# A two-block hybrid layer on one Trainium2 core: level exponents of the recurrent mixer by TensorE in place of GpSimd

## The chip, the cores and the metric

One core of a Trainium2 chip runs the whole program. The time is that of the device for one execution, in microseconds (us); the numbers below are medians of several executions. The engines of a core each run their own queue in order and meet at semaphores: TensorE (PE in the profile, with its weight loads as PEld), VectorE (DVE), ScalarE (ACT), GpSimd (POOL) and SyncE (SP), which here issues the transfers.

## The reference

Two layers follow one another on 2048 tokens of width 1024. Only the second one's mixers matter here. It projects x to 3784 columns, then two mixers run: an attention over 256 selected keys per query (4 heads, an index score of 8 heads, a top-k by threshold), and a gated linear recurrence with 4 heads of 128 key and 128 value channels. Of the recurrence:

```python
f = lbh + (1.0 - lbh) * jax.nn.sigmoid(f_raw)      # decay per token, head and key channel
k = 1.0 - f
log_f = jnp.log(f)
bc = jnp.cumsum(log_f, over the tokens of a chunk)
diff = bn[:, :, :, None, :] - bn[:, :, None, :, :]
decay = jnp.exp(jnp.where(causal, diff, -jnp.inf))
scores = einsum('bhtk,bhsk,bhtsk->bhts', qn, kn, decay)
o = scores @ vn + (qn * exp(bn)) @ state
state = exp(b_last) * state + (kn * exp(b_last - bn)).T @ vn
```

The decay between two tokens s < t is different for each key channel, so the scores are no plain matrix product of q and k. Then come an RMS norm, a gate, the output projection and a layer norm.

## The kernel before

The second layer's mixers run in eighteen steps (`second_mixers`, L3456), each closed by a barrier of all engines (`step`, L145). Step k has up to five branches that share no data within the step: index scores of one tile of 128 queries (`index_scores`), the upper half of the search for the threshold (`upper_half`, 16 rounds on VectorE), the lower half (`lower_half`, 16 rounds on ScalarE), the attention of a tile (`attend`) and one chunk of 128 tokens of the recurrence (`hgrn_chunk`, in steps 0 to 15). Tiles are taken from the widest to the narrowest: the last query tile sees 2048 keys, each later step 128 fewer, while a chunk of the recurrence is always the same work. So steps shorten from 123 to 50 us.

Within a step the order on each engine is settled when the program is built. Each branch is written as a generator per engine that yields a place between 0 and 1 before each piece of work (`yield 8.4 / N`), and `together` (L162) puts the pieces of all branches on the engine's queue in order of their places. The recurrence counts its places in 29ths of a step (`N = 29.0`). The queues are in order, so a piece that waits holds up whatever stands behind it.

The recurrence of a chunk divides the pairs s < t into seven levels. At level l blocks of 2 * 2^l tokens are halved; a pair is of that level when s lies in the first half and t in the second. With b the running sum of log f and j the last token of the first half, the decay is exp(b_j - b_s) * exp(b_t - b_j), and both factors are at most 1. So for each level the kernel needs an exponent E for every token and channel: b_j - b_s in first halves, b_t - b_j in second ones. Then:

- TensorE makes b as a product of log f with a matrix of ones (`c.upto`, L3275) in accumulator bank 6, and ScalarE copies it to SBUF (`bT`, L3154).
- GpSimd makes the exponents of a level with two subtractions of 256 columns, `diffs` (L3185, L3186), and b_last - b for the state with one of 512 columns (L3198).
- ScalarE takes the exponential of a level in place (L3158), and those of b_last - b and b (L3162 to L3165).
- GpSimd multiplies first halves with k and second halves with q, `tilde` (L3191, L3192).
- TensorE multiplies the result with itself, per head (L3293), into bank 6 or 7 by turns; that holds the level's scores at the pairs of the level.
- VectorE picks these into A with a mask, `pick` (L3241).

E has two buffers and the banks 6 and 7 serve two levels by turns. In GpSimd's queue the subtractions of level l+1 stand ahead of the products of level l. TensorE writes a bank again when VectorE has picked the level two before.

After the levels the state is read and updated (L3300 to L3312, L3257) and the output is normed. The other branches' work on the same queues: TensorE has index dots (L2718), logits (L3053), turns (L3059) and weighing (L3066); ScalarE has rectifying (L2702), signs (L2814), exponentials (L2961) and copies (L2976); VectorE has the weighted sum of index scores (L2681), counting (L2774 to L2778), and adding the mask and taking the maximum (L2991); GpSimd has the bias (L2942).

A setup (`last_mixers_setup`, L3322) ahead of the eighteen steps loads constants and turns keys.

Of the kernel before, what the change touches and what calls it, by code (L numbers as in the profile page):

```python
# [17 lines left out]
ALU = mybir.AluOpType  # L18
# [3 lines left out]
P = 128  # L22
# [31 lines left out]
BD = 128  # L54
PAD = 4
GROUP = 512
LEVELS = 7
# [39 lines left out]
CONST_COLS = CAUSAL0 + GROUP + 2 * P  # L97

# [2493 lines left out]
HGRN_SIGNALS = ("hx_in hf_ahead sigs h_tanhs h_silus f_done logf turned_hq hq_kept turned_hk hk_kept sums b_kept pairs own_set "  # L2592
# [480 lines left out]
def hgrn_buffers(B, big, y):  # L3073
# [11 lines left out]
    b.bT = B.sb("bT", [P, H, P])  # L3085
# [17 lines left out]
def hgrn_chunk(c, b, s, proj, i):  # L3103
# [5 lines left out]
    lb, g, state, x, k, qT, kT, bT, E, A = b.lb, b.g, b.state, b.x, b.k, b.hqT, b.kT, b.bT, b.E, b.A  # L3109
# [12 lines left out]

    def joint(l):
        half = 1 << l
        v = bT[:].rearrange("p h (n a b) -> p h n a b", a=2, b=half)[:, :, :, 0, half - 1]
        return spread(v, 3, half)
# [10 lines left out]
    def scalar(act):  # L3137
# [16 lines left out]
        act.activation(bT[:], four(6), ACT.Copy).then_inc(s.b_kept, 1)  # L3154
        for l in range(LEVELS):
            yield (6.5 + 2 * l) / N
            act.wait_ge(s.diffs, 2 * (l + 1))
            act.activation(E[:, l % 2], E[:, l % 2], ACT.Exp).then_inc(s.h_exps, 1)  # L3158
            if l == 0:
                yield 7.2 / N  # L3160
                act.wait_ge(s.e_in, 1)
                act.activation(ke[:], ke[:], ACT.Exp)  # L3162
                act.drain()
                act.activation(qe[:], bT[:], ACT.Exp)
                act.activation(dec[:], bT[:, :, P - 1], ACT.Exp).then_inc(s.e_out, 1)  # L3165
# [12 lines left out]
    def gpsimd(pool):  # L3178

        def diffs(l):  # L3180
            if l >= 2:

                pool.wait_ge(s.pairs, l)
            (e0, e1), (b0, b1) = halves(E[:, l % 2], l), halves(bT[:], l)
            pool.tensor_tensor(e0, joint(l), b0, ALU.subtract).then_inc(s.diffs, 1)  # L3185
            pool.tensor_tensor(e1, b1, joint(l), ALU.subtract).then_inc(s.diffs, 1)  # L3186

# [6 lines left out]
        yield 6 / N  # L3194
        pool.wait_ge(s.b_kept, 1)
        diffs(0)

        pool.tensor_tensor(ke[:], spread(bT[:, :, P - 1], 2, P), bT[:], ALU.subtract).then_inc(s.e_in, 1)  # L3198
        for l in range(LEVELS):
            if l + 1 < LEVELS:  # L3200
                yield (7 + 2 * l) / N
                diffs(l + 1)
            yield (7.5 + 2 * l) / N
            tilde(l)
# [409 lines left out]
```

## Time and profile before

| | us |
|---|---|
| median of 3 runs | 5201.58 |
| lowest and highest | 5184.79, 5215.15 |
| span of the profiled execution (first to last instruction) | 5189.6 |
| PE busy | 4361.9 (84%) |
| DVE busy | 2639.9 (51%) |
| ACT busy | 1922.0 (37%) |
| POOL busy | 711.8 (14%) |

The profile gives the profiled execution as its span; what the timed runs have beyond a span (start and end of the execution) is not split off. The shares are means over stages that differ much: the first layer and the two projections are TensorE's, while in the stage that the change touches (3469 to 4932 us of the span) VectorE and ScalarE are busy as well. The mean granted TensorE clock was 0.829 of full speed over the span.

### The profile page before, as it was taken

How to read it: one execution, taken by the hardware profiler on the slowest of the kernel's cores; microseconds unless marked ns; L12 is line 12 of the kernel's file. 1: busy time of each engine (PE TensorE's matmuls, PEld its weight loads, DVE VectorE, ACT ScalarE, POOL GpSimd, SP SyncE). 2: the span in 40 equal slices, each digit the busy share in tenths (PEclk: the TensorE clock that was granted, in tenths of full speed). 3: DMA queues.
4: the chain of work that ended last, by engine and by line, in shares of the span. 5: the costliest groups of instructions: out<-in, count | busy, mean ns of one | idle time of the engine just before them, and what ended most of it. 6: DMA issues, size and time to landing. Idle time of an engine off the chain costs nothing. (4 is left out here: it accounts for less than half of the span.)

```text
span 5189.6 us, 65192 instructions
## 1 busy us (share of the span) xinstructions
PE 4361.9 (84%) x23554; PEld 3247.0 (63%) x23554; DVE 2639.9 (51%) x5371; ACT 1922.0 (37%) x3900; POOL 711.8 (14%) x745
## 2 busy tenths in 40 slices
PE   7997999984688888888898999977787878787679
PEld 6885777774566555656787888853344444454467
DVE  3113444445555544444212111138889888888545
ACT  3112323324323333333101101023667776777621
POOL 3102111100000000000000000003222333344400
PEclk9998999985567777778899999976677788778789
DMA  5327666664000000000423212120000000101033
GB/s 184 119 106 239 210 221 204 215 206 139 28 24 24 24 24 24 13 24 3 154 109 115 82 65 81 55 73 17 19 28 29 19 19 19 37 19 35 31 126 118
DMA packets 203393, 425.84 MB, mean 82 GB/s; under 512 B 37224, under 2 KB 67596, under 8 KB 202908
## 3 DMA queue, kind: packets, MB, share of 16 engines
q1 hardware_dynamic: 203072, 421.67, 23.7%
q8 instruction: 188, 3.08, 0.2%
q14 instruction: 133, 1.09, 0.1%
HBM read 299.93 MB, written 121.65 MB: 81 GB/s over the span
## 5 line engine op out<-in xcount | busy, mean ns | idle before, releaser
L3185 POOL TENSOR_TENSOR ds_E<-ds_bT 128x256 f32<-128x256 f32 x112 | 72.8, 650 | 2797.5 <-ACT ds_bT L3154 2620.6
L2718 PE MATMUL ds_big<-ds_ikT,ds_iqT 64*128 64x512 f32 (+3 forms) x608 | 382.0, 759 | 75.4 <-ACT ds_iqT L2695 54.6
L301 PE MATMUL g_acc<-g_ws_hi,g_hT_hi 128*128 128x512 f32 (+1 forms) x1024 | 386.5, 377 | 0.0
L303 PE MATMUL g_acc<-g_ws_hi,g_hT_lo 128*128 128x512 f32 (+1 forms) x1024 | 384.9, 376 | 0.0
L302 PE MATMUL g_acc<-g_ws_lo,g_hT_hi 128*128 128x512 f32 (+1 forms) x1024 | 384.9, 376 | 0.0
L529 PE MATMUL mm_big<-mm_gw_hi,mm_ghT_hi 128*128 128x512 f32 (+1 forms) x768 | 321.4, 418 | 31.0 <-PEq L134 31.0
L2774 DVE TENSOR_SCALAR_CACHE_REDUCE ds_seen<-ds_eq,ds_num 128x2048 uint16<-128x2048 uint16 (+13 forms) x224 | 331.3, 1479 | 26.4 <-issue 4.4
L531 PE MATMUL mm_big<-mm_gw_hi,mm_ghT_lo 128*128 128x512 f32 (+1 forms) x768 | 302.7, 394 | 0.0
L530 PE MATMUL mm_big<-mm_gw_lo,mm_ghT_hi 128*128 128x512 f32 (+1 forms) x768 | 302.0, 393 | 0.0
L2814 ACT ACTIVATE ds_signs<-ds_lo,ds_at 128x2048 bf16<-128x2048 uint16 (+13 forms) x224 | 291.3, 1301 | 1.5
L328 DVE COPY g_stage<-g_acc 128x512 f32<-128x512 f32 (+1 forms) x64 | 41.5, 649 | 459.2 <-PE g_acc L303 459.2
L2681 DVE SCALAR_TENSOR_TENSOR ds_score<-ds_rel,ds_iw,ds_score 128x512 f32<-128x512 f32 (+3 forms) x266 | 221.3, 836 | 56.5 <-ACT ds_rel L2702 39.8
L1332 PE MATMUL fox_big<-fox_kT,fox_qT 65*128 65x512 f32 (+3 forms) x320 | 223.7, 793 | 29.9 <-PEq L134 29.9
L2718 PEld LDWEIGHTS ds_big<-ds_ikT,ds_iqT 64*128 64x128 f32 x608 | 107.6, 233 | 208.7 <-issue 76.0
L2702 ACT ACTIVATE ds_rel<-ds_big 128x512 f32<-128x512 f32 (+3 forms) x304 | 162.6, 538 | 168.1 <-PE ds_big L2718 89.0
L3293 PEld LDWEIGHTS ds_big<-ds_E 128*128 128x128 f32 x896 | 137.4, 234 | 138.0 <-POOL ds_E L3192 71.5
L347 ACT ACTIVATE g_stage<-g_acc 128x512 f32<-128x512 f32 (+1 forms) x64 | 36.2, 566 | 502.5 <-PE g_acc L303 502.5
L303 PEld LDWEIGHTS g_acc<-g_ws_hi,g_hT_lo 128*128 128x128 f32 x1024 | 193.5, 189 | 35.4
L302 PEld LDWEIGHTS g_acc<-g_ws_lo,g_hT_hi 128*128 128x128 f32 x1024 | 193.7, 189 | 34.9
L301 PEld LDWEIGHTS g_acc<-g_ws_hi,g_hT_hi 128*128 128x128 f32 x1024 | 193.8, 189 | 34.7
L1288 ACT ACTIVATE fox_pT<-fox_big 128x512 f32<-128x512 f32 (+3 forms) x160 | 85.2, 533 | 347.8 <-PE fox_big L1356 347.7
L3066 PE MATMUL ds_big<-ds_pT,ds_ct 128*128 128x128 f32 x1088 | 171.6, 303 | 49.6 <-ACT ds_pT L2976 49.4
(519 smaller groups left out, 10155.1 us busy)
## 6 DMA issues: line engine op xcount, KB each, us to landing
mm_ghT_hi<-turned SPq DMA_DIRECT2D x96, 512.0 KB, 3.8
mm_ghT_lo<-turned SPq DMA_DIRECT2D x96, 512.0 KB, 5.5
proj<-g_stage SPq DMA_DIRECT2D x112, 256.0 KB, 2.0
proj<-mm_gstage SPq DMA_DIRECT2D x80, 256.0 KB, 5.0
mm_x<-proj SPq DMA_DIRECT2D x64, 256.0 KB, 3.8
second_raw<-in_w_in SPq DMA_DIRECT2D x56, 256.0 KB, 4.2
proj<-fp_stage SPq DMA_DIRECT2D x48, 256.0 KB, 2.0
mm_graw<-in_w_in SPq DMA_DIRECT2D x40, 256.0 KB, 6.4
```

What stands on the lines that cost most here:

```text
L301: pe.matmul(sums, hT.hi[:, k, tile], wt.hi[:, k, 0:width], start=(k == 0), stop=False)
L302: pe.matmul(sums, hT.hi[:, k, tile], wt.lo[:, k, 0:width], start=False, stop=False)
L303: mm = pe.matmul(sums, hT.lo[:, k, tile], wt.hi[:, k, 0:width], start=False, stop=(k == KD - 1))
L529: pe.matmul(sums, b.hT.hi[:, u % 3, k], wt.hi[:, k, 0:width], start=(k == 0), stop=False)
L530: pe.matmul(sums, b.hT.hi[:, u % 3, k], wt.lo[:, k, 0:width], start=False, stop=False)
L531: m = pe.matmul(sums, b.hT.lo[:, u % 3, k], wt.hi[:, k, 0:width], start=False, stop=(k == KD - 1))
L1332: pe.matmul(big[:, n, 0:wd], b.qT[:, h, k * P:(k + 1) * P], b.kT[:, h, x:x + wd], start=True, stop=True).then_inc(s.logits, 1)
L2681: d = dve.scalar_tensor_tensor(out=score[:, x:x + wd], in0=rel[:, n % 2, 0:wd], scalar=sg, in1=score[:, x:x + wd], op0=ALU.mult, op1=ALU.add)
L2718: pe.matmul(big[:, n % 2, 0:wd], iqT[o, h // 2], b.ikT[o, x:x + wd], start=True, stop=True)\
L2774: dve.tensor_scalar(seen, hi, cand, 0.0, ALU.is_ge, ALU.add, accum_out=count)
L2814: act.activation(signs, lo, ACT.Sign, bias=now, accum_out=sums[:, bit:bit + 1])
L3066: m = pe.matmul(big[:, 5, h * P:(h + 1) * P], b.ct[:, x // P + t], pT[:, (h * NP + p) % 2, t], start=(p == 0 and t == 0), stop=(x + (t + 1 ...
```

## The change

The exponents of a level no longer come from differences of b. Each is a sum of log f over some tokens: over s+1 to j for a token s of a first half, over j+1 to t for a token t of a second half. So for each level TensorE multiplies log f (as it lies, tokens on the partitions) with a 128 x 128 matrix of zeros and ones. The seven matrices are made on the host, come in as an input `sums` and stay in SBUF. b_last - b is made likewise, with the constant matrix `c.after`. The product goes to bank 6 or 7, the same bank that the level's scores use later; ScalarE reads the exponents there and writes E to SBUF. `bT` and its copy go. In TensorE's queue the exponents of level l+1 stand ahead of the scores of level l, and wait for VectorE's pick of level l-1; that pick moves from place 9.3 + 2l to 7.9 + 2l. ScalarE's exponentials of b and b_last - b come ahead of all levels.

```diff
+def level_sums():
+    s, t = np.arange(P)[:, None], np.arange(P)[None, :]
+    out = []
+    for l in range(LEVELS):
+        half = 1 << l
+        joint = t // (2 * half) * (2 * half) + half - 1
+        out.append(((t < s) & (s <= joint)) | ((joint < s) & (s <= t)))
+    return np.concatenate(out, axis=1).astype(np.float32)
...
     def scalar(act):
         act.wait_ge(s.sums, 1)
-        act.activation(bT[:], four(6), ACT.Copy).then_inc(s.b_kept, 1)
+        act.activation(qe[:], four(6), ACT.Exp)
+        act.activation(dec[:], four(6)[:, :, P - 1], ACT.Exp).then_inc(s.e_out, 1)
+        yield 4.6 / N
+        act.wait_ge(s.e_in, 1)
+        act.activation(ke[:], four(7), ACT.Exp).then_inc(s.ke_kept, 1)
         for l in range(LEVELS):
-            yield (6.5 + 2 * l) / N
-            act.wait_ge(s.diffs, 2 * (l + 1))
-            act.activation(E[:, l % 2], E[:, l % 2], ACT.Exp).then_inc(s.h_exps, 1)
-            if l == 0:
-                yield 7.2 / N
-                act.wait_ge(s.e_in, 1)
-                act.activation(ke[:], ke[:], ACT.Exp)
-                act.drain()
-                act.activation(qe[:], bT[:], ACT.Exp)
-                act.activation(dec[:], bT[:, :, P - 1], ACT.Exp).then_inc(s.e_out, 1)
+            yield (6.6 + 2 * l) / N
+            act.wait_ge(s.diffs, l + 1)
+            act.activation(E[:, l % 2], four(6 + l % 2), ACT.Exp).then_inc(s.h_exps, 1)
...
     def gpsimd(pool):
-        def diffs(l):
-            if l >= 2:
-                pool.wait_ge(s.pairs, l)
-            (e0, e1), (b0, b1) = halves(E[:, l % 2], l), halves(bT[:], l)
-            pool.tensor_tensor(e0, joint(l), b0, ALU.subtract).then_inc(s.diffs, 1)
-            pool.tensor_tensor(e1, b1, joint(l), ALU.subtract).then_inc(s.diffs, 1)
-        yield 6 / N
-        pool.wait_ge(s.b_kept, 1)
-        diffs(0)
-        pool.tensor_tensor(ke[:], spread(bT[:, :, P - 1], 2, P), bT[:], ALU.subtract).then_inc(s.e_in, 1)
         for l in range(LEVELS):
-            if l + 1 < LEVELS:
-                yield (7 + 2 * l) / N
-                diffs(l + 1)
             yield (7.5 + 2 * l) / N
             tilde(l)
         yield 20 / N
-        pool.wait_ge(s.e_out, 1)
+        pool.wait_ge(s.ke_kept, 1)
...
     def vector(dve):
             if l:
-                yield (9.3 + 2 * l) / N
+                yield (7.9 + 2 * l) / N
                 pick(l - 1)
...
+    def diffs(pe, l):
+        if l == 0:
+            pe.wait_ge(s.e_out, 1)
+        elif l == 1:
+            pe.wait_ge(s.own_set, 1)
+        else:
+            pe.wait_ge(s.picked, l - 1)
+        for h in range(H):
+            m = pe.matmul(big[:, 6 + l % 2, h * P:(h + 1) * P], f[:, h * BD:(h + 1) * BD], b.sums[:, l],
+                          start=True, stop=True)
+        m.then_inc(s.diffs, 1)
     def tensor(pe):
         m.then_inc(s.sums, 1)
+        yield 4.2 / N
+        pe.wait_ge(s.hk_kept, 1)
+        for h in range(H):
+            m = pe.matmul(big[:, 7, h * P:(h + 1) * P], f[:, h * BD:(h + 1) * BD], c.after, start=True, stop=True)
+        m.then_inc(s.e_in, 1)
         yield 5 / N
-        pe.wait_ge(s.hk_kept, 1)
+        diffs(pe, 0)
+        pe.wait_ge(s.ke_kept, 1)
         for h in range(H):
             m = pe.matmul(big[:, 7, h * P:(h + 1) * P], kT[:, h], qT[:, h], start=True, stop=True)
         m.then_inc(s.pairs, 1)
         for l in range(LEVELS):
+            if l + 1 < LEVELS:
+                yield (8.2 + 2 * l) / N
+                diffs(pe, l + 1)
             yield (8.4 + 2 * l) / N
             pe.wait_ge(s.tilde, 2 * (l + 1))
-            if l == 0:
-                pe.wait_ge(s.b_kept, 1)
-            elif l == 1:
-                pe.wait_ge(s.own_set, 1)
-            else:
-                pe.wait_ge(s.picked, l - 1)
...
 def last_mixers_setup(nc, c, w, proj, table, onehot, sums, ib, tb, ab, hb):
             sp.dma_start(hg[:], row(w['hgrn_norm_g_2'])).then_inc(s.lb_in, 16)
+            sp.dma_start(hb.sums[:].rearrange("p l t -> p (l t)"), sums).then_inc(s.rest_in, 16)
```

## Rows read from the trace of the kernel before

**Rows 1.** Windows by step: stretch, length, busy PE, PEld, DVE, ACT, POOL, clock, DMA.
```profile
3763.00:3886.00 123.00, 104.04 (x420) 59.53 (x420) 108.80 (x188) 88.18 (x156) 35.52 (x38) 0.79 0.06 20
...
4000.00:4116.00 116.00, 97.33 (x385) 55.73 (x385) 100.94 (x182) 81.40 (x149) 34.66 (x40) 0.77 0.07 24
...
4746.50:4817.00 70.50, 48.85 (x236) 34.54 (x236) 56.11 (x147) 51.19 (x124) 31.73 (x38) 0.81 0.09 31
4817.00:4882.00 65.00, 39.44 (x208) 31.89 (x208) 44.41 (x133) 45.02 (x115) 31.41 (x39) 0.74 0.09 33
4882.00:4932.00 50.00, 28.30 (x135) 21.69 (x133) 16.73 (x41) 38.16 (x97) 27.29 (x35) 0.66 0.11 38
...
sum 1511.00, PE 1158.77 PEld 702.42 DVE 1232.47 ACT 1016.99 POOL 531.46; mean PE 68.16 PEld 41.32 DVE 72.50 ACT 59.82 POOL 31.26
```

**Rows 2.** Waits, 3540 to 4595 us: waiter, releaser, total us, times, longest.
```profile
DVE ds_score L2681 <- ACT ds_rel L2702: 18.9, 16, 3.8
...
PE ds_big L2718 <- ACT ds_iqT L2695: 43.9, 10, 5.2
PE ds_big L3019 <- PEq L134: 34.1, 11, 5.3
```

**Rows 3.** Groups by form, GpSimd: shapes xcount, busy us, mean ns, idle before.
```profile
L3186 POOL TENSOR_TENSOR ds_E<-ds_bT 128x256 f32<-128x256 f32 x112 | 76.4, 682 | 0.0
L3185 POOL TENSOR_TENSOR ds_E<-ds_bT 128x256 f32<-128x256 f32 x112 | 72.8, 650 | 2797.5 <-ACT ds_bT L3154 2620.6 <-PE ds_big L3293 176.8
...
L3198 POOL TENSOR_TENSOR ds_ke<-ds_bT 128x512 f32<-128x512 f32 x16 | 18.6, 1162 | 0.0
```

**Rows 4.** VectorE: groups by form, then timeline (start us, us, engine, line).
```profile
L2681 DVE SCALAR_TENSOR_TENSOR ds_score<-ds_rel,ds_iw,ds_score 128x512 f32<-128x512 f32 x196 | 180.4, 923 | 49.0 <-ACT ds_rel L2702 37.8 <-issue 0.6
L2778 DVE SCALAR_TENSOR_TENSOR ds_num<-ds_num 128x1 f32<-128x1 f32 x224 | 54.4, 243 | 19.4 <-issue 3.0
...
3950.99 0.16 DVE L2778 SCALAR_TENSOR_TENSOR ds_num<-ds_num 128x1 f32<-128x1 f32 x1
...
3951.61 0.61 POOL L3185 TENSOR_TENSOR ds_E<-ds_bT 128x256 f32<-128x256 f32 x1 [3.53 <-PE ds_big L3293]
...
3951.80 0.97 DVE L2681 SCALAR_TENSOR_TENSOR ds_score<-ds_rel,ds_iw,ds_score 128x512 f32<-128x512 f32 x1
...
3956.60 0.73 DVE L2681 SCALAR_TENSOR_TENSOR ds_score<-ds_rel,ds_iw,ds_score 128x512 f32<-128x512 f32 x1
```

**Rows 5.** Groups by form, ScalarE: a level's exponential and the copy.
```profile
L3158 ACT ACTIVATE ds_E<-ds_E 128x512 f32<-128x512 f32 x112 | 69.9, 624 | 4.7 <-POOL ds_E L3186 2.9
...
L3154 ACT ACTIVATE ds_bT<-ds_big 128x512 f32<-128x512 f32 x16 | 9.5, 596 | 4.1 <-PE ds_big L3275 3.4
```

**Rows 6.** TensorE's level scores: group by form, and two of them in the timeline.
```profile
L3293 PE MATMUL ds_big<-ds_E 128*128 128x128 f32 x896 | 158.5, 332 | 60.7 <-POOL ds_E L3192 40.1 <-DVE ds_A L3241 20.3
...
3950.37 1.16 PE L3293 MATMUL ds_big<-ds_E 128*128 128x128 f32 x8
...
4777.33 2.08 PE L3293 MATMUL ds_big<-ds_E 128*128 128x128 f32 x8 [1.79 <-POOL ds_E L3192]
```

**Rows 7.** Timeline, step from 3886: scores of level 4, pick of level 3.
```profile
3960.27 1.16 PE L3293 MATMUL ds_big<-ds_E 128*128 128x128 f32 x8
...
3963.13 0.74 DVE L3241 COPY_PREDICATED ds_A<-consts_sb,ds_big 128x512 f32<-128x512 uint32 x1
```

**Rows 8.** Timeline, last recurrent step, around the exponential of the last level.
```profile
4925.53 1.02 PE L3053 MATMUL ds_big<-ds_cT,ds_ql 128*128 128x512 f32 x2
...
4926.11 0.63 ACT L3158 ACTIVATE ds_E<-ds_E 128x512 f32<-128x512 f32 x1 [1.40 <-POOL ds_E L3186]
...
4927.53 0.72 POOL L3191 TENSOR_TENSOR ds_E<-ds_E,ds_kT 128x256 f32<-128x256 f32 x1
```

**Rows 9.** Timeline, setup: SyncE's last load and VectorE's last arithmetic.
```profile
3443.21 0.56 SPq L3349 DMA_DIRECT2D ds_uv<-in_w_uv  x1
...
3471.16 0.42 DVE L3390 TENSOR_SCALAR ds_hg<-ds_hg 128x512 f32<-128x512 f32 x1
```

More of the change, by code:

```diff
@@ L2591 @@
                   "o_kept o_ps y_done ")
-HGRN_SIGNALS = ("hx_in hf_ahead sigs h_tanhs h_silus f_done logf turned_hq hq_kept turned_hk hk_kept sums b_kept pairs own_set "
+HGRN_SIGNALS = ("hx_in hf_ahead sigs h_tanhs h_silus f_done logf turned_hq hq_kept turned_hk hk_kept sums ke_kept pairs own_set "
                 "diffs h_exps tilde picked e_in e_out ee_done ke_t ktok_done ho_ps up_ps sqd rs hy_done ")
@@ L3084, in hgrn_buffers @@
     b.hqT = B.sb("hqT", [P, H, P])
-    b.bT = B.sb("bT", [P, H, P])
+    b.sums = B.sb("hsums", [P, LEVELS, P])
     b.E = B.sb("E", [P, 2, H, P])
@@ L3108, in hgrn_chunk @@
     H = BH
-    lb, g, state, x, k, qT, kT, bT, E, A = b.lb, b.g, b.state, b.x, b.k, b.hqT, b.kT, b.bT, b.E, b.A
+    lb, g, state, x, k, qT, kT, E, A = b.lb, b.g, b.state, b.x, b.k, b.hqT, b.kT, b.E, b.A
     qe, ke, ktok, dec, ss, big = b.qe, b.ke, b.ktok, b.dec, b.ss, b.big
@@ L3121, in halves @@
         return v[:, :, :, 0], v[:, :, :, 1]
[L3123 to L3126, printed above, removed]
     def sync(sp):
@@ L3316, in hgrn_chunk, with last_mixers_setup @@
     return {"sync": sync, "gpsimd": gpsimd, "vector": vector, "scalar": scalar, "tensor": tensor}
-def last_mixers_setup(nc, c, w, proj, table, onehot, ib, tb, ab, hb):
+def last_mixers_setup(nc, c, w, proj, table, onehot, sums, ib, tb, ab, hb):
     R, big = P, hb.big
@@ L3351, in _ @@
             sp.dma_start(table, ot).then_inc(s.table_out, 16)
-            sp.wait_ge(s.rest_in, n + 32)
+            sp.wait_ge(s.rest_in, n + 48)
             sp.wait_ge(s.table_out, 16)
@@ L3453, with second_mixers @@
 LAST_SIGNALS = "pw_in0 pw_in1 pw_in2 pw_hi pw_lo "
-def second_mixers(nc, c, w, proj, mix, table, onehot, x_old, out):
+def second_mixers(nc, c, w, proj, mix, table, onehot, sums, x_old, out):
     H, R, KEEP = 4, 128, float(TOPK)
@@ L3482, in second_mixers @@
         hb = hgrn_buffers(E, big, y)
-        last_mixers_setup(nc, c, w, proj, table, onehot, ib, tb, ab, hb)
+        last_mixers_setup(nc, c, w, proj, table, onehot, sums, ib, tb, ab, hb)
         last = Named()
@@ L3555, in second_mixers, with program @@
         project_out(nc, c, mix, w['w_o_2'], x_old, out, "pf", ln=(w['ln_g_2'], w['ln_b_2']), held=last)
-def program(nc, t, consts, onehot, out):
+def program(nc, t, consts, onehot, sums, out):
     w = {n: (v[0] if v.shape[0] == 1 else v) for n, v in t.items()}
@@ L3583, in program @@
             second_projection(nc, c, x2, w['w_in_2'], proj2, spans((0, COLS2)), raw)
-        second_mixers(nc, c, w, proj2, mixed2, table, onehot, x2, out)
+        second_mixers(nc, c, w, proj2, mixed2, table, onehot, sums, x2, out)
     nc.sync.sem_clear(nc.turns.ranges[1 - nc.turns.now])
@@ L3603 @@
         views[n] = nc.dram_tensor(f"in_{n}", a.shape, F32, kind="ExternalInput").ap()
-    made = {"consts": shape_constants(), "onehot": bucket_table()}
+    made = {"consts": shape_constants(), "onehot": bucket_table(), "sums": level_sums()}
     for n, a in made.items():
@@ L3608 @@
     out = nc.dram_tensor("out", [1, SEQ, D_MODEL], F32, kind="ExternalOutput").ap()
-    program(nc, {n: views[n] for n in INPUTS}, views["consts"], views["onehot"], out)
+    program(nc, {n: views[n] for n in INPUTS}, views["consts"], views["onehot"], views["sums"], out)
     r = run_bass_kernel_spmd(nc, [arrays], core_ids=[0])
```

## The prediction

> **What bounds the kernel now.** The touched code runs only in the last-but-one stage, so I read that first: the busy times of its sixteen recurrent steps [rows 1]. The reader is to see three kinds of step. From 3540 to about 4675 us VectorE is busy for 85 to 91% of each step (100.94 of 116.00 us in one) and TensorE for 75 to 85%; GpSimd, whose work the change removes, has 34.66 us in that step. In the last two, VectorE falls to 44.41 and 16.73 us, and no engine is full: these are bound by latency, by chains that go from engine to engine. Next, who waits: over ten long steps the longest entry of VectorE's waits is 18.9 us in 1055 us [rows 2]. VectorE is the limit there; what shortens VectorE shortens the step, and what shortens GpSimd alone doesn't. Third, TensorE at the start of a step: 43.9 us for ten waits on the turned index queries and 34.1 us for eleven step barriers, so 4.4 + 3.1 = 7.5 us of each step that it can't use [rows 2].
>
> About 0.5%, 26 us, is what a measurement of this kernel tells from no change. The stage is 1463 us long (the 1511 us of the windows less the 48 after the last recurrent step), so it would have to move by 1.8%.
>
> **GpSimd's part that goes.** Per chunk, seven times two subtractions and one wide one: 72.8 + 76.4 + 18.6 = 167.8 us over sixteen chunks [rows 3], 10.5 us a chunk, of GpSimd's 531.46 us in the stage [rows 1]. It is worth something through two doors.
>
> First, VectorE is slower beside GpSimd. VectorE's weighted sum of 512 columns takes 0.73 us with GpSimd quiet and 0.97 us when issued 0.19 us behind a GpSimd subtraction [rows 4]; its mean over 196 is 923 ns, so 196 x 0.193 = 37.8 us are lost to company. A one-column operation takes 0.16 us alone and 243 ns in the mean of 224: 18.6 us more. Together 56 us. The removed instructions are 167.8/531.46 = 32% of GpSimd's time, so 18 us of it, if the loss is spread by time. The other short VectorE operations that are delayed stand at the beginning and end of a step, beside GpSimd work that stays, so I add nothing for them. The lower bound is 0 (the remaining GpSimd work slides into the freed places and hurts as before), the upper one twice, 36 us. Of the 18 us, thirteen of sixteen steps can turn it into time: **-15 us**.
>
> The Trainium skill (SBUF — State Buffer, section Who interferes with whom) has the reason: a VectorE operation with two inputs in SBUF and a GpSimd operation that reads SBUF take a common port pair as an exclusive lock, and the second waits for the first. The 0.97 against 0.73 us agrees. By that rule alone a collision would cost up to a whole GpSimd instruction (0.61 us), where the mean loss here is 0.19 us, as most do not collide. If each removed instruction blocked VectorE for half its length, 84 us would go (an estimate by the page's rule and the lengths in the trace); the 56 us that the rows show for all of GpSimd forbid that.
>
> Second, latency. GpSimd's queue has the subtractions of level l+1 before the products of level l. In the long steps nobody on the path waits for it: 0. In the short ones it shortens a chain, but the exponents then come from another queue (below), so I count 0, bound -1.3 us a step (two subtractions, 0.65 + 0.68) in five steps.
>
> **ScalarE.** One copy of 596 ns goes [rows 5] and one drain; the three exponentials remain, read from the accumulators in place of SBUF. The nearest rows: a copy out of the accumulators takes 596 ns and an exponential in SBUF 624 ns, so I count the new form as the old; bound 28 ns each either way, 0.3 us a chunk. 16 x 0.6 = 9.5 us of an engine that is 70% busy (81.40 of 116.00): 0 on the path, bound -9.5.
>
> **TensorE's part that comes.** Eight groups a chunk (seven levels and the one for the keys' decay), each four products of 128x128x128 in f32, which the trace shows as eight matmuls. The same shape is there: the level scores take 1.16 us a group at the upper clock level (2.4 GHz) and 2.08 us at the lower (1.2 GHz), and 158.5/112 = 1.42 us in the mean [rows 6]. So 8 x 1.42 = 11.3 us a chunk (9.3 at the upper, 16.6 at the lower level), 181 us over the stage. Room: in the step of 116 us TensorE has 97.33 busy and 7.5 shut off, 11.2 us left; in the first with attention at full width 104.04 of 123.00, 11.5 left [rows 1, 2]. It just fits. TensorE isn't at its peak, though: the granted clock is 0.77 to 0.79 in these two, so over 40% of the time it runs at half speed, and work done at that speed would shrink. I take 0.5 us for each of ten long steps for VectorE instructions that are now late behind a full TensorE: **+5 us**; bounds 0 and the rival below.
>
> **The waits that are added.** The products of level l+1 stand at place 8.2+2l of 29 in TensorE's order and wait until VectorE has picked level l-1; VectorE's pick moves from 9.3+2l to 7.9+2l for this. While TensorE waits, index scores, logits and turns queue behind it, and VectorE in the end waits for those. In the step from 3886 (the 114 us up to the one of row 4000): the pick of level 3 started at 3963.13 [rows 7] at place 17.3. A unit is 114/29 = 3.9 us, so 1.4 units earlier is 3957.6, done by 3958.4. TensorE reaches the point just before the scores of level 4, which started at 3960.27; less a group of 1.16 us the new one must begin at 3959.1. The pick comes 0.7 us before that. So the wait is nearly always over, but with little to spare: 0 in the long steps. VectorE's own earlier place is safe: the scores of level 3 started at 3950.37 [rows 6], some 7 us before.
>
> **The short steps.** ScalarE's exponential of a level (place 6.6+2l) is now 0.4 units behind TensorE's products (6.2+2l): 0.7 us in a step of 50 us, less than a group takes. In the last recurrent step: TensorE finished logits at 4925.53 + 1.02 = 4926.55 and would make the last level's exponents then, until 4927.71, while the exponential started at 4926.11 [rows 8]. It would start at 4927.8, GpSimd's products of the level at 4928.5 in place of 4927.53: 1.0 us late, and the level scores after them too. I take +1.0 us for each of the last five steps: **+5 us**; bounds -1.3 (GpSimd's relief counts in full) and +3 (the group at the lower clock level on two levels).
>
> **Beginning.** The matrices come in with one more transfer of 128 x 3584 B = 459 KB in the setup; the queue issued its last load at 3443.21 and VectorE ends the setup 28 us later, at 3471.16 + 0.42 [rows 9]: hidden, 0. It moves six other loads by about the 0.56 us that one issue takes; what ends the setup, VectorE's arithmetic on the bounds, waits for none of them. Bound +0.6.
>
> **Sum.** -15 + 5 + 5 = -5 us. The page gives the span of the profiled execution, 5189.6 us, which would become 5184.6; the median of the timed runs is 12 us above the span, and the difference is what I carry over: 5201.58 - 5 = **5197 us**. No measurable change is likeliest.
>
> **Rival A, slower: TensorE becomes the limit.** If the new groups run at the lower clock level, they add 16.6 us a step. Then TensorE's busy time, the addition and the 7.5 us shut off exceed the step: by 97.33 + 16.6 + 7.5 - 116 = 5.4 us, by 2.5 us in the one of 70.5 us; over the eleven steps from 3763 to 4817 (the first and the last of which stand in [rows 1]) it is 51 us in all. With the +5 of the short steps and no relief, as VectorE isn't the limit then: 5201.6 + 56 = 5258 us. It decides once a group costs more than 1.4 us in these steps (8 x 1.4 = 11.2, the room above). For it: the room is that small. Against it: the scores of levels 3 and 4 in a long step ran at 1.16 us [rows 6, 7]. Halfway, a third of the steps, gives 5225.
> The Trainium skill (TensorE: Matmul & The Clock Gate, What's actually happening) says that the half clock is the default and activity releases it. The clock of 0.77 to 0.79 beside 84% busy doesn't bear that out cleanly; if it holds, 64 more matmuls a step raise the clock and this rival dies.
>
> **Rival B, faster.** The removed subtractions sit between VectorE's densest work, and all of the upper bound counts: -36 us x 13/16 = -29, nothing late on TensorE as more work keeps its clock up, and the short steps gain GpSimd's 1.3 us each: -6.5. Together 5166 us. For it: the 0.97 us stood beside a subtraction that goes [rows 4]. Against it: 531.46 - 167.8 = 364 us of GpSimd's work stay and can collide [rows 1, 3].
>
> **Rival C: it is only moved.** GpSimd's remaining work collides as often as before, TensorE hides everything: 5202 +- 5. It can't be told from my forecast by time.
>
> **Chances.** Forecast with C 0.56, A in whole or part 0.25, B 0.19. These are the chances of same, slower and faster. The range takes in B to 5163 and half of A to 5230.
>
> **What would show it.** VectorE's weighted sum falls from 923 ns towards 850 (right) or stays (C). GpSimd's busy time falls by 168 us. TensorE's rises by 150 to 260 us; the mean of a new group at 1.2 us speaks for B, at 2 us for A, and so does a VectorE that waits over 5 us a step on ScalarE's rectified scores. The last two steps grow by 1 us. I am wrong if TensorE's waits for the pick total over 30 us, or if a long step changes by more than 3 us.

## The result and the profile after

The changed kernel takes 5211.37 us (median of 20 runs, 5197.08 to 5222.88) against 5194.70 us for the kernel before in the same comparison. The ratio is 1.0029 with a 95% interval of 1.0018 to 1.0039: 15 us slower, 9 to 20. The forecast was 5 us faster, no measurable change; the size is below the 26 us that the prediction took for measurable, the sign is wrong, and twenty runs tell it.

First the whole stage, in one window each, from the barrier ahead of the first recurrent step to the one behind the last (length, busy of PE, PEld, DVE, ACT, POOL, clock). In the kernel before that last barrier stands at 4942.6 us. The windows read ahead of the prediction closed the step at 4932, when its state was still being read: it is 61 us long and not 50, and the stage 1470.7 us and not 1463. The kernel before:

```profile
3471.90:4942.60 1470.70, 1139.43 (x4608) 689.20 (x4608) 1215.19 (x2392) 1000.44 (x2046) 525.51 (x604) 0.76 0.07 26
```

The changed kernel:

```profile
3474.90:4966.00 1491.10, 1197.47 (x5632) 793.31 (x5632) 1177.34 (x2392) 991.98 (x2030) 364.20 (x364) 0.81 0.07 25
```

The stage holds the loss: it is 20.4 us longer, of the 24.0 us between the two profiled executions. VectorE, the limit of the long steps, is busy for 37.9 us less, twice what was forecast, and GpSimd for 161 us less. VectorE's idle time rises by 58 us, from 255.5 to 313.8, and eats that and more. TensorE is busy for only 58.0 us more. The new work is far larger than this; the changed kernel's groups by form, TensorE:

```profile
L2730 PE MATMUL ds_big<-ds_ikT,ds_iqT 64*128 64x512 f32 x448 | 298.6, 782 | 70.7 <-ACT ds_iqT L2707 52.6 <-ACT ds_rel L2714 18.0
L3257 PE MATMUL ds_big<-ds_hsums,ds_f 128*128 128x128 f32 x896 | 149.0, 317 | 46.6 <-DVE ds_A L3229 45.7 <-DVE ds_A L3235 0.8
L3296 PE MATMUL ds_big<-ds_E 128*128 128x128 f32 x896 | 139.1, 305 | 8.4 <-POOL ds_E L3188 8.1
L3281 PE MATMUL ds_big<-consts_sb,ds_f 128*128 128x128 f32 x128 | 31.7, 429 | 0.0
```

149.0 + 31.7 = 180.7 us are new, as forecast (181). But the old work shrank, the level scores from 158.5 to 139.1 us [rows 6] and, of others, the index dots from 315.7 us in the kernel before:

```profile
L2718 PE MATMUL ds_big<-ds_ikT,ds_iqT 64*128 64x512 f32 x448 | 315.7, 836 | 70.7 <-ACT ds_iqT L2695 51.5 <-ACT ds_rel L2702 19.1
```

The reader is to see two thirds of the added busy time given back, at a granted clock of 0.81 in place of 0.76. Cut at each change of the granted clock, TensorE's busy time before is 538 us at the lower level and 601 at the upper; after, it is 412 and 785, with 80 and 101 us of the new groups among them. So 206 us of old work left the lower level; taken at half the time on the upper one [rows 6 have 2.08 and 1.16 us], that is some 103 of the 123 us that are missing. The rest is overlap: group by group, busy times add up to 107 us more than the total before, and to 129 us more after. The relief of VectorE, changed kernel, groups by form, against [rows 4]:

```profile
L2693 DVE SCALAR_TENSOR_TENSOR ds_score<-ds_rel,ds_iw,ds_score 128x512 f32<-128x512 f32 x196 | 158.5, 811 | 55.3 <-ACT ds_rel L2714 44.5 <-issue 0.6
L2790 DVE SCALAR_TENSOR_TENSOR ds_num<-ds_num 128x1 f32<-128x1 f32 x224 | 43.6, 194 | 19.1 <-issue 2.6
```

923 ns became 811, 243 became 194. The 923 of this one profile is high, though: five kernels below that keep all of GpSimd's work (twice, twicemid and the three with earlier picks in the kernel before) have 881 to 895. Then who waits for whom (total us, times, longest), first VectorE in the kernel before:

```profile
DVE ds_score L2681 <- ACT ds_rel L2702: 39.8, 31, 3.8
DVE ds_L L2991 <- PE ds_big L3053: 20.8, 24, 2.8
DVE ds_A L3247 <- PE ds_big L3280: 17.4, 8, 8.8
...
DVE ds_A L3241 <- PE ds_big L3293: 11.3, 4, 4.2
```

In the changed kernel VectorE waits for the same four, and others for each other in two new ways:

```profile
DVE ds_score L2693 <- ACT ds_rel L2714: 51.1, 36, 5.3
DVE ds_A L3235 <- PE ds_big L3287: 41.9, 15, 10.5
DVE ds_A L3229 <- PE ds_big L3296: 23.7, 16, 4.2
DVE ds_L L3003 <- PE ds_big L3065: 22.9, 24, 3.3
...
ACT ds_E L3169 <- PE ds_big L3257: 67.1, 35, 4.6
...
PE ds_big L3257 <- DVE ds_A L3229: 45.7, 41, 5.2
```

Own scores (k with q of the same token; L3235 is the line L3247 of before) cost 24.5 us more, picks 12.4, rectified scores 11.3. TensorE's matmuls sit idle 45.7 us in front of the level exponents until a pick, and ScalarE waits 67.1 us for these exponents. Of the wait for picks, most is in the long steps (3540 to 4600 us):

```profile
PE ds_big L3257 <- DVE ds_A L3229: 35.5, 28, 5.2
```

By chunk, the largest change of a single one stands at the beginning. The first chunk, which has index scores beside it and no attention, from barrier to barrier, before and after:

```profile
3471.90:3541.20 69.30, 57.71 (x184) 26.97 (x184) 42.00 (x61) 32.78 (x64) 30.62 (x34) 0.80 0.10 35
```

```profile
3474.90:3550.80 75.90, 66.53 (x248) 36.30 (x248) 40.17 (x61) 32.85 (x63) 19.01 (x19) 0.79 0.09 32
```

6.6 us of the 20 are here, 4.4 in chunks 1 and 2, 7.8 in chunks 11 to 15. Chunks 3 to 10, the long steps from 3763 to 4593, sum up to within 2 us of what they were. Single ones moved by up to 6 us; but chunk 4, which did, is 5 us longer in bpick79 and bpick86 too, so no cause is read from them one by one.

### The profile page after: what moved, and what is told of

It reads as the page before. It is cut to its first block and busy times, and to the rows that moved or that the text cites. A ratio compares the mean times of both kernels' runs of the same rounds, so it can differ in the third digit from the quotient of the medians.

```text
span 5213.6 us, 66857 instructions
## 1 busy us (share of the span) xinstructions
PE 4416.9 (85%) x24578; PEld 3349.1 (64%) x24578; DVE 2604.5 (50%) x5371; ACT 1912.6 (37%) x3884; POOL 551.0 (11%) x505
## 5 line engine op out<-in xcount | busy, mean ns | idle before, releaser
L2730 PE MATMUL ds_big<-ds_ikT,ds_iqT 64*128 64x512 f32 (+3 forms) x608 | 355.6, 697 | 76.0 <-ACT ds_iqT L2707 56.6
L3187 POOL TENSOR_TENSOR ds_E<-ds_E,ds_kT 128x256 f32<-128x256 f32 x112 | 90.6, 809 | 3107.7 <-ACT ds_E L3169 3107.6
L2693 DVE SCALAR_TENSOR_TENSOR ds_score<-ds_rel,ds_iw,ds_score 128x512 f32<-128x512 f32 (+3 forms) x266 | 204.0, 768 | 67.4 <-ACT ds_rel L2714 51.1
L3257 PEld LDWEIGHTS ds_big<-ds_hsums,ds_f 128*128 128x128 f32 x896 | 128.4, 219 | 122.9 <-DVE ds_A L3229 80.4
L1057 PE MATMUL fp_acc<-fp_ws_hi,fp_hT_hi 128*128 128x512 f32 (+1 forms) x528 | 199.0, 377 | 9.0 <-issue 3.9
```

The costliest lines, as they stand in the source:

```text
L1057: pe.matmul(sums, hT.hi[:, j % 3, n], ws.hi[:, n, at], start=(n == 0), stop=False)
L2693: d = dve.scalar_tensor_tensor(out=score[:, x:x + wd], in0=rel[:, n % 2, 0:wd], scalar=sg, in1=score[:, x:x + wd], op0=ALU.mult, op1=ALU.add)
L2730: pe.matmul(big[:, n % 2, 0:wd], iqT[o, h // 2], b.ikT[o, x:x + wd], start=True, stop=True)\
```

## The experiments

All ratios are against the kernel before, run in turns on the same chip; 0.001 is 5.2 us. The medians of the kernel before differ by up to 7 us between comparisons, so only ratios are compared. Two questions came first: is it the load on TensorE, or the waits that come with it?

| kernel | ratio | 95% interval | us against before |
|---|---|---|---|
| the change | 1.0029 | 1.0018 to 1.0039 | +15 |
| twice: load only | 1.0053 | 1.0040 to 1.0066 | +27 |
| nodiff: relief only | 0.9967 | 0.9953 to 0.9980 | -17 |
| nodifftwice: relief and load | 0.9990 | 0.9972 to 1.0009 | -5 |
| twicemid: load in chunks 1 to 10 | 1.0023 | 1.0008 to 1.0037 | +12 |
| onehead: the change, a third of its load | 1.0006 | 0.9995 to 1.0016 | +3 |
| pick71: the change, picks earlier | 1.0011 | 0.9999 to 1.0024 | +6 |
| pick75: the same, by half | 1.0006 | 0.9991 to 1.0021 | +3 |
| own76: the change, own scores used later | 1.0037 | 1.0021 to 1.0054 | +19 |
| own76pick71: both | 1.0038 | 1.0021 to 1.0054 | +20 |
| kelate: pick75, one group behind the own scores | 0.9986 | 0.9975 to 0.9997 | -7 |
| exp70: pick75, ScalarE later | 1.0025 | 1.0012 to 1.0037 | +13 |
| kelate_exp70: both | 0.9982 | 0.9969 to 0.9995 | -9 |
| bpick79: before, picks earlier | 0.9986 | 0.9974 to 0.9998 | -7 |
| bpick86: before, picks earlier by half | 1.0001 | 0.9985 to 1.0017 | 0 |
| bown76pick79: before, both places | 0.9995 | 0.9983 to 1.0007 | -3 |

The us of a row are uncertain by 5 to 10, and a difference of two rows by 8 to 13.

Where the time lies, by the profiles: us between barriers, as the difference from the kernel before, whose own lengths are in the first row. Each is one execution. Kelate's was its fastest (5171.13 us, median 5184.15), nodiff's its slowest (5184.33, median 5172.53). The same code takes 65.1 to 69.3 us in chunk 0 (twicemid and the kernel before), but the same within 0.4 us elsewhere (twice and twicemid in chunks 1 to 10).

| kernel | chunk 0 | 1 and 2 | 3 to 10 | 11 to 15 | all |
|---|---|---|---|---|---|
| before, length | 69.3 | 222.3 | 829.9 | 349.2 | 1470.7 |
| the change | +6.6 | +4.4 | +1.6 | +7.8 | +20.4 |
| twice | +1.7 | +3.0 | +12.3 | +11.9 | +28.9 |
| twicemid | -4.2 | +2.6 | +12.3 | -0.1 | +10.6 |
| nodiff | -7.3 | -3.1 | -3.8 | -2.9 | -17.1 |
| nodifftwice | +0.4 | +0.5 | +2.3 | -3.6 | -0.4 |
| pick71 | +6.0 | -0.3 | -8.2 | +9.8 | +7.3 |
| pick75 | +4.1 | -0.8 | -2.1 | +8.2 | +9.4 |
| kelate | -0.3 | +2.6 | -7.5 | -7.3 | -12.5 |
| kelate_exp70 | -0.5 | -3.7 | -8.1 | +5.5 | -6.8 |

**Load alone (twice).** The score products of the kernel before, each level's and the own ones, are issued twice (at the own scores, L3280, the edit is the same).

```diff
-            for h in range(H):
+            for h in [*range(H), *range(H)]:
                 m = pe.matmul(big[:, 6 + l % 2, h * P:(h + 1) * P], E[:, l % 2, h], E[:, l % 2, h],
```

> The kernel before, with the four products of each level's scores, and of the own scores, issued twice: eight more groups a chunk on TensorE, as the change has, but no new wait and GpSimd's subtractions kept. If TensorE's load costs the time (load theory): 20 to 35 us slower than before (the change's 15 us loss plus the relief of VectorE that it doesn't have). If the new waits cost it (wait theory): 0 to 8 us slower than before, TensorE's busy time up by 150 to 180 us.

27 us slower (21 to 34): load costs, and more than the change loses. The stage's window and the scores of this kernel:

```profile
3468.80:4968.40 1499.60, 1193.52 (x5632) 791.30 (x5632) 1205.11 (x2392) 1000.35 (x2046) 525.04 (x604) 0.81 0.07 25
```

```profile
L3293 PE MATMUL ds_big<-ds_E 128*128 128x128 f32 x1792 | 261.2, 306 | 65.8 <-POOL ds_E L3192 50.1 <-DVE ds_A L3241 15.6
```

TensorE's busy time rose by 54 us in all, not the 150 to 180 expected, although the level scores alone rose by 103 us [rows 6]; the clock went to 0.81 here too. A busy time that grows by 54 us in a stage of 1471, 77% busy, still makes it 29 us longer. How full TensorE is doesn't set the price: in chunks 11 to 15, where it is 68% busy in the kernel before, 320 more matmuls cost 12 us, in chunks 3 to 10, 81% busy, 512 cost 12 us. That the price is set by where the products stand in the queue is the likely reading; this run doesn't show it.

**Relief alone (nodiff).**

```diff
-            act.wait_ge(s.diffs, 2 * (l + 1))
-            act.activation(E[:, l % 2], E[:, l % 2], ACT.Exp).then_inc(s.h_exps, 1)
+            if l >= 2:
+                act.wait_ge(s.pairs, l)
+            act.activation(E[:, l % 2], bT[:], ACT.Exp).then_inc(s.h_exps, 1)
...
-                act.wait_ge(s.e_in, 1)
-                act.activation(ke[:], ke[:], ACT.Exp)
+                act.activation(ke[:], bT[:], ACT.Exp)
...
-        diffs(0)
...
-        pool.tensor_tensor(ke[:], spread(bT[:, :, P - 1], 2, P), bT[:], ALU.subtract).then_inc(s.e_in, 1)
...
-                diffs(l + 1)
```

> The kernel before without GpSimd's fifteen subtractions of a chunk: ScalarE takes the exponentials from the copied running sum, so the level exponents are left out of the computation. Nothing is added to TensorE. This is the change's gain by itself. VectorE's busy time in the stage fell by 38 us in the changed kernel; if that is worth its time, 25 to 38 us faster than before. By the forecast's term 15 us faster. If the relief is no use as VectorE waits instead: within 5 us of before.

17 us faster (10 to 24), near the forecast's 15; the 25 to 38 us expected from VectorE's busy time did not come. Its weighted sum fell to 861 ns only:

```profile
L2681 DVE SCALAR_TENSOR_TENSOR ds_score<-ds_rel,ds_iw,ds_score 128x512 f32<-128x512 f32 x196 | 168.2, 861 | 46.5 <-ACT ds_rel L2702 35.5 <-issue 0.6
```

Why it falls further, to 811, in the changed kernel, no run shows. Nodiff's edit also takes GpSimd out of the chain that leads to a level's exponential, so a faster VectorE and a shorter chain aren't told apart here. And the gain isn't where it was looked for: 7.3 of the 17 us are in chunk 0, where the granted clock was 0.86 for 0.80, and 6.9 in chunks 1 to 10.

**Both, without the change's waits (nodifftwice).** The two edits above together.

> The kernel before without GpSimd's subtractions (ScalarE takes the exponentials of the copied running sum, so the level exponents are left out) and with every group of score products issued twice: the change's relief and the change's load, without its new waits and its new order. If the two add up: -17 + 27 = 10 us slower than before, so about 5 us faster than the changed kernel, and like the changed kernel with earlier picks (6 us slower than before). If the relief pays for the load by giving VectorE slack: 0 to 4 us slower than before. If 15 us or more slower: the new waits cost nothing.

-5 us (-15 to +5), not +10: with the relief, the same load costs 12 us in place of 27, though these two are hardly told apart (15 us, uncertain by 14). So the changed kernel, at +15, has 20 us (9 to 31) that belong to its new waits and its new order. In the profiles these are 6.2 us in chunk 0, 3.9 in chunks 1 and 2 and 11.4 in chunks 11 to 15; in chunks 3 to 10 there are none.

**Where the load costs (twicemid).**

```diff
-            for h in [*range(H), *range(H)]:
+            for h in (list(range(H)) * (2 if 1 <= i <= 10 else 1)):
```

> The kernel before with the score products issued twice in chunks 1 to 10 only, the long steps, 640 of the 1024 added matmuls. If TensorE's load costs in the long steps, where it is 75 to 85% busy: 15 to 22 us slower than before. If it costs in the short steps, where the chain from engine to engine sets the end: 0 to 8 us slower, and the other 20 us of the twice run belong to chunks 0 and 11 to 15.

12 us for 640 matmuls, between the two expectations; the other 384, in chunks 0 and 11 to 15, cost the other 15 of twice's 27. In proportion it would be 17 and 10, which these times can't exclude. The profiles are finer: chunks 1 to 10 are 15 us longer in both kernels, 24 ns a matmul, and chunks 11 to 15 are 12 us longer in twice, 37 ns a matmul, and as before in twicemid. So load is dearer where the chain sets the end, and not free in either place.

**The waits with a third of the load (onehead).**

```diff
-        for h in range(H):
+        for h in range(1):
             m = pe.matmul(big[:, 6 + l % 2, h * P:(h + 1) * P], f[:, h * BD:(h + 1) * BD], b.sums[:, l],
...
-            act.activation(E[:, l % 2], four(6 + l % 2), ACT.Exp).then_inc(s.h_exps, 1)
+            act.activation(E[:, l % 2], spread(four(6 + l % 2)[:, 0], 1, H), ACT.Exp).then_inc(s.h_exps, 1)
```

> The changed kernel with a level's exponents made for one of the four heads only and used for all (so three quarters of the level exponents are left out of the computation). All waits and orders stay; 672 of the 1024 added matmuls go. If load costs what the twice run showed (27 us for 1024 matmuls), this is 18 us faster than the changed kernel, some 3 us faster than before. If the added waits carry the loss: within 6 us of the changed kernel, so 10 us or more slower than before.

+3 us, 12 less than the change and between the two expectations; nodiff, without load or new waits, is at -17. Of these 20 us (uncertain by 9) a third of the load takes 4 to 9, at 12 to 27 us for the whole, and the waits and the order leave 11 to 16.

**The wait for the pick (pick71, pick75).** Only VectorE's place moves.

```diff
-                yield (7.9 + 2 * l) / N
+                yield (7.1 + 2 * l) / N
                 pick(l - 1)
```

> The changed kernel with VectorE's picks at place 7.1+2l in place of 7.9+2l, 3 us earlier in a long step; the work is the same. Wait theory: TensorE's waits for the pick (126 us idle in 92 cases in the changed kernel) fall to under 60 us and the time falls by 8 to 20 us against the changed kernel, so within 10 us of before. Load theory: it stays 10 to 20 us slower than before.

> The changed kernel with picks at 7.5+2l, between the 7.9 of the change and the 7.1 that gave 9 us. If TensorE's wait for the pick is what it gives back: 3 to 9 us faster than the changed kernel, TensorE's idle for the pick between 59 and 126 us. If it is luck of one order: anywhere within 8 us of the changed kernel.

+6 and +3 us, so 9 and 12 us of the change's loss come back, each uncertain by 9. TensorE's idle time in front of the exponents, matmuls only, in pick71:

```profile
PE ds_big L3257 <- DVE ds_A L3229: 18.6, 19, 3.2
```

and in pick75:

```profile
PE ds_big L3257 <- DVE ds_A L3229: 32.1, 29, 4.2
```

45.7, 32.1 and 18.6 us with places 7.9, 7.5 and 7.1. (The 126 us in the expectations is the view that adds weight loads, 80.4, to matmuls, 45.7: one idle time seen by two queues. By that view 7.5 has 92.1 us and 7.1 has 59.) In the profiles the gain is in the long steps: chunks 3 to 10 take 9.8 us less in pick71 and 3.7 in pick75 than in the change. VectorE pays at the other end: in pick71 its picks wait 43.1 us for scores, against 23.7, so 7.1 isn't better than 7.5.

**The kernel before with earlier picks (bpick79, bpick86).** The same edit, 9.3 to 7.9 or 8.6.

> The kernel before with only the pick's place changed, 9.3+2l to 7.9+2l. Wait and load theories: within 5 us of before, since the scores are ready several us before the pick in the long steps. A third theory, that the earlier place itself makes VectorE wait for scores: 8 us or more slower, with VectorE waits on the level scores up from 11 us to over 20 us.

> The kernel before with picks at 8.6+2l, halfway to 7.9+2l. If the 7 us gained with 7.9 are an effect of picks no longer holding up TensorE: 3 to 7 us faster than before. If they are luck of one order: anywhere within 8 us of before.

-7 and 0 us. The earlier place does no harm by itself, so the pick's move is not what the change loses by. Halfway gave nothing; the gain at 7.9 may be luck of one order.

**The head of a step (own76, own76pick71, bown76pick79).** In a step's beginning the change puts two groups ahead of the own scores. These experiments only let VectorE come later.

```diff
-        yield 6 / N
+        yield 7.6 / N

         dve.wait_ge(s.pairs, 1)
```

> The changed kernel with VectorE's first use of the own scores at place 7.6 in place of 6. In the changed kernel VectorE waits 41.9 us there in 15 cases (17.4 us in 4 before), as TensorE makes two groups ahead of them now. If this head of the step is part of the loss: that wait under 15 us and 5 to 15 us faster than the changed kernel. If VectorE only waits elsewhere instead: within 3 us of the changed kernel.

> Both places moved: own scores at 7.6, picks at 7.1+2l. If the two waits are separate losses: 9 us (pick) and 5 to 15 us (own) add up, so 0 to 10 us faster than before. If the load is what is left: 3 to 8 us slower than before, as with the picks alone.

> The kernel before with own scores at 7.6 and picks at 7.9+2l, no other change. If waiting for own scores costs VectorE time before too (17.4 us in 4 cases): 7 to 15 us faster than before, better than the 7 us of the picks alone. If these waits lie in short steps where VectorE isn't the limit: the same 7 us as with the picks alone.

+19, +20 and -3 us. In own76 the second reading fits: the wait fell and came up elsewhere at once, and the time stayed (4 us more than the change, uncertain by 10). The other two expectations are misses. Own76:

```profile
DVE ds_score L2693 <- ACT ds_rel L2714: 56.6, 34, 4.6
DVE ds_L L3003 <- PE ds_big L3065: 45.2, 32, 4.3
...
DVE ds_A L3235 <- PE ds_big L3287: 11.4, 2, 10.8
```

41.9 to 11.4 us at the own scores, 22.9 to 45.2 at the logits. (The 17.4 us of the kernel before are 8 waits, not the 4 that the expectations name.) Moving the one who waits didn't help while TensorE was late. Why both places together lose what the pick alone gains is open.

**The order at the head (kelate).** With picks at 7.5+2l, the group for b_last - b goes behind the own scores, and level 0's exponents too; ScalarE takes the exponential of b_last - b behind that of level 0. Level 1's exponents now wait for that exponential and not for the own scores' use. These moves come in one edit and weren't tried one by one.

```diff
-        yield 4.6 / N
-        act.wait_ge(s.e_in, 1)
-        act.activation(ke[:], four(7), ACT.Exp).then_inc(s.ke_kept, 1)
...
+            if l == 0:
+                yield 7.4 / N
+                act.wait_ge(s.e_in, 1)
+                act.activation(ke[:], four(7), ACT.Exp).then_inc(s.ke_kept, 1)
...
-            pe.wait_ge(s.own_set, 1)
+            pe.wait_ge(s.ke_kept, 1)
...
-        yield 4.2 / N
-        pe.wait_ge(s.hk_kept, 1)
-        for h in range(H):
-            m = pe.matmul(big[:, 7, h * P:(h + 1) * P], f[:, h * BD:(h + 1) * BD], c.after, start=True, stop=True)
-        m.then_inc(s.e_in, 1)
         yield 5 / N
-        diffs(pe, 0)
-        pe.wait_ge(s.ke_kept, 1)
+        pe.wait_ge(s.hk_kept, 1)
...
         m.then_inc(s.pairs, 1)
+        diffs(pe, 0)
+        yield 7 / N
+        pe.wait_ge(s.own_set, 1)
+        for h in range(H):
+            m = pe.matmul(big[:, 7, h * P:(h + 1) * P], f[:, h * BD:(h + 1) * BD], c.after, start=True, stop=True)
+        m.then_inc(s.e_in, 1)
```

> The changed kernel with picks at 7.5+2l and the group for b_last - b, with its exponential, moved behind the own scores; the own scores no longer wait for that exponential, level 0's exponents come after them. If the head of the step holds the rest: VectorE's wait for own scores falls from 43 us to under 25, chunk 0 is 3 us or more shorter, and the time is 4 to 10 us less than with the picks alone (3 us slower than before), so 1 to 7 us faster than before. If it doesn't: within 3 us of the picks alone.

-7 us: 22 less than the change (14 to 30) and 10 less than pick75 (0 to 20), with the three signs of the first reading. VectorE's wait for own scores, kelate:

```profile
DVE ds_A L3236 <- PE ds_big L3282: 18.6, 9, 8.8
```

43.1 us in pick75, 18.6 here, 17.4 in the kernel before. The first chunk, and its head in the timeline (start us, us, line), kelate:

```profile
3462.90:3531.90 69.00, 60.27 (x248) 32.44 (x248) 39.30 (x61) 32.61 (x63) 18.55 (x19) 0.87 0.10 35
```

```profile
3474.47 2.05 PE L3277 MATMUL ds_big<-consts_sb,ds_f 128*128 128x128 f32 x8
3476.45 2.08 PE L2730 MATMUL ds_big<-ds_ikT,ds_iqT 64*128 64x512 f32 x4
3478.46 1.90 PE L3282 MATMUL ds_big<-ds_hqT,ds_kT 128*128 128x128 f32 x8
3480.09 0.97 PEld L3258 LDWEIGHTS ds_big<-ds_hsums,ds_f 128*128 128x128 f32 x8
3480.20 1.06 PE L3258 MATMUL ds_big<-ds_hsums,ds_f 128*128 128x128 f32 x8
3480.40 0.69 DVE L3236 TENSOR_TENSOR ds_A<-ds_big,consts_sb 128x512 f32<-128x512 f32 x1 [0.39 <-PE ds_big L3282]
```

The changed kernel at the same point:

```profile
3486.52 2.04 PE L3276 MATMUL ds_big<-consts_sb,ds_f 128*128 128x128 f32 x8
3488.50 2.07 PE L2730 MATMUL ds_big<-ds_ikT,ds_iqT 64*128 64x512 f32 x2
...
3490.50 2.08 PE L3281 MATMUL ds_big<-consts_sb,ds_f 128*128 128x128 f32 x8
...
3492.50 2.07 PE L2730 MATMUL ds_big<-ds_ikT,ds_iqT 64*128 64x512 f32 x2
...
3494.51 2.07 PE L3257 MATMUL ds_big<-ds_hsums,ds_f 128*128 128x128 f32 x8
...
3496.37 1.91 PE L3287 MATMUL ds_big<-ds_hqT,ds_kT 128*128 128x128 f32 x8
...
3498.32 0.69 DVE L3235 TENSOR_TENSOR ds_A<-ds_big,consts_sb 128x512 f32<-128x512 f32 x1 [6.27 <-PE ds_big L3287]
```

From the running sum to the own scores in VectorE: 11.8 us in the change, 5.9 in kelate. TensorE works without a gap at the lower clock level, about 2 us a group, and VectorE is idle 6.27 us in front of the own scores; index scores queue behind. In kelate the first chunk is 69.0 us long, as before (69.3), and not 75.9. That repeats: 72.9 to 75.9 us in the six profiles with the change's head and its whole load, 69.0 and 68.8 in the two with kelate's.

The clock goes with the order. From the barrier on, TensorE has the lower level for 17.4 us in the kernel before, for 17.2 in kelate, and for 24.9 in the change. Kelate:

```profile
3462.90:3480.10 17.20, 14.97 (x38) 7.57 (x39) 7.17 (x16) 9.87 (x16) 0.00 (x0) 0.50 0.39 137
```

and the change:

```profile
3474.90:3499.80 24.90, 22.62 (x58) 12.18 (x58) 8.26 (x18) 10.56 (x17) 0.00 (x0) 0.50 0.27 95
```

The own scores' delay of 5.9 us arises at the lower level in both, so it is the order's; what the later rise of the clock adds in the rest of the chunk isn't separated.

Beyond chunk 0 the head's part isn't shown. Most of what kelate's profile has over pick75's is in chunks 11 to 15 (15.5 us), and kelate_exp70, with the same head, is 5.5 us longer there than the kernel before.

**ScalarE's wait (exp70, kelate_exp70).** ScalarE's exponentials move from 6.6+2l to 7.0+2l.

```diff
-            yield (6.6 + 2 * l) / N
+            yield (7 + 2 * l) / N
```

> The changed kernel with picks at 7.5+2l and ScalarE's exponentials at 7.0+2l in place of 6.6+2l. If ScalarE's waits for the exponents (55 us in 35 cases) hold up the rectified scores and so VectorE: that wait under 30 us and 3 to 8 us faster than with the picks alone. If they are idle time that costs nothing: within 3 us.

> Both. If both hold a part: 8 to 15 us faster than with the picks alone, so 5 to 12 us faster than before, and the fastest complete kernel of the study beside the 7 us of the kernel before with earlier picks. If neither does: within 4 us of the picks alone.

+13 us without kelate's order, 10 worse than pick75 (0 to 20); with it -9, which can't be told from kelate's -7. The first is outside both expectations; the second, 12 us less than pick75, is inside "both hold a part", but exp70 by itself speaks against that reading. ScalarE's waits for exponents fell from 55 us to this:

```profile
ACT ds_E L3169 <- PE ds_big L3257: 30.9, 18, 3.9
```

So less of that idle time bought nothing, and a later exponential may cost. kelate_exp70 has the lowest ratio of the complete kernels, 0.9982 (0.9969 to 0.9995). bpick79, a single number changed in the kernel before, has 0.9986 (0.9974 to 0.9998), which can't be told from it, so the change of engine isn't needed for that gain.

## Why the prediction was wrong

The step that failed is "The waits that are added", which the sum has at 0, and with it the order at the head of a step, which the prediction never looks at. The runs put 20 us (9 to 31) on the two together: the change is at +15, and nodifftwice, with a load of the same size and the relief but the old waits and order, at -5. That nodifftwice lands on the forecast of -5 is luck. Its parts are -17 and +12, where the sum has -15 and +5, and +5 for a delay that nodifftwice doesn't have.

*VectorE's limit in the long steps and the share of GpSimd.* The size held: -15 us was forecast for the relief, nodiff measured -17 (10 to 24). The place didn't. The 15 us were to come from steps in which VectorE is the limit; in nodiff's profile chunks 1 to 10 give 6.9 us of 17, and chunk 0 gives 7.3 at a higher clock. So the agreement is in part luck, and how much of the 17 is VectorE's is open. VectorE's busy time fell by 37.9 us in the change, above the upper bound of 36. That overstates: nodiff alone gives 861 ns for the weighted sum, and kernels with all of GpSimd's work have 881 to 895 beside the 923 of the profile that was read.

*TensorE's added work.* The size held (180.7 us against 181). The term **+5 us** for "VectorE instructions that are now late behind a full TensorE" was too small if anything: the load costs 12 us (0 to 24) with the relief, 27 without. The bookkeeping behind it failed more clearly: room was read as the step's length less busy time, and that room didn't run out, as total busy time rose by 58 us only. TensorE's queue is in order, so a group delays whatever stands behind it by its own 1.1 to 2 us. The head of chunk 0 shows that; for the other places it is argued. Rival A named the right engine with the wrong mechanism. In its eleven steps the level exponents took 98.34 us and the group for b_last - b 21.64 (busy of PE and PEld, clock):

```profile
3778.20:4838.30 1060.10, 98.34 (x616) 84.66 (x616) 0.84 0.07 25
3778.20:4838.30 1060.10, 21.64 (x88) 19.84 (x88) 0.84 0.07 25
```

That is 120.0/88 = 1.36 us a group, just below its point of 1.4, and the clock rose.

*The new wait for the pick.* "0 in the long steps" failed. It was worked out for one level of one step, with a margin of 0.7 us; over all, TensorE's matmuls were idle 45.7 us in 41 cases, above the 30 us that I had named as proof of being wrong, and 35.5 us of them in the long steps. Earlier picks return 9 to 12 us (uncertain by 9). What the wait costs by itself in the long steps is less clear: chunks 3 to 10 are no longer in the change than in nodifftwice, and yet pick71 is 9.8 us shorter there.

*The head of the step.* Not in the prediction at all. It counted eight groups a chunk and looked at levels and at the last ones, but never at what the group for b_last - b and level 0's exponents delay: the own scores, with VectorE's wait for them up from 17.4 to 41.9 us. Not all of that is the two groups ahead of them. Nodifftwice has none ahead, only own scores issued twice, and its wait for them is:

```profile
DVE ds_A L3239 <- PE ds_big L3272: 31.9, 13, 8.6
```

Kelate, with the whole load and the own scores first, waits 18.6. Earlier picks and the new head together are worth 22 us (14 to 30, kelate against the change), enough for the sign of the result. The parts seem to add up, -5 for relief and load, 9 to 12 for the pick and 10 for the head, to 14 to 17 against 15 measured; but the first already has part of the wait for own scores, and each is uncertain by about 10, so that sum proves nothing.

*The short steps.* +5 us, 1 for each of the last five, forecast. In the profiles chunks 11 to 15 are 7.8 us longer, of which chunk 13 alone has 5.1, and the last two have 0.2 and 2.1. With the same exponents in TensorE, kelate is 7.3 us shorter there than the kernel before and kelate_exp70 5.5 us longer, so what is order here and what is the price of the method is open.

*ScalarE and the beginning.* Held: ScalarE has 8.5 us less to do and it shows in no time; the exponential out of the accumulators takes 597 ns at the median against 622. The setup is 0.5 us shorter, not longer.

What stays open: why own76pick71 is 14 us (uncertain by 11) behind pick71, and how much of any order's 5 us is luck, as bpick79 and bpick86 suggest.

## What to carry to other kernels

Work moved to an engine with room can be paid for at its place in that engine's queue. List what stands behind each new instruction, at the head of the stage above all, where here TensorE ran at its lower clock and VectorE waited for its first results; a group that nobody needs soon (here that for b_last - b) goes behind those that someone waits for. A margin worked out for one place of a repeated wait says little: read the wait at all its places before it is put at zero.

## What the runs showed of the hardware

TensorE gave back most of what was added: with 1024 matmuls more in a stage, busy time rose by 58 us where the new groups take 180.7 us, at a granted clock of 0.81 for 0.76 (54 us with the load alone). Busy time at the lower clock level fell from 538 to 412 us, and that explains some 103 of the 123 us. VectorE's busy time for the same instructions differs between profiles by order alone, 881 to 923 ns for its weighted sum with all of GpSimd's work in place, so a gain must be larger than that spread before it is read as relief. And moving one engine's place by 0.4 to 1.6 of 29 units, with no work changed, moved this kernel by up to 14 us (uncertain by 11).
